# Feed-forward block of an encoder layer: the up projection of two token groups as seven half products, and the down projection as a phase of its own

## The reference

```
h  = h + mixed @ w_out
n2 = rmsnorm(h, ffn_norm)
u  = dwconv3(n2 @ w_up, conv_w, conv_b)      # width 3 along the tokens, each sequence by itself
a, g = split(u, 2)                           # 2816 features each
h  = h + (a * gelu_tanh(g)) @ w_down
gate = sigmoid(rmsnorm(h, ple_norm) @ w_ple_gate)
h  = h + gate * (p @ w_ple)
y  = rmsnorm(h, final_norm)
```

## Time and profile before

| | us |
|---|---|
| median of three runs | 2175.13 |
| lowest, highest | 2174.33, 2176.18 |
| the profiled execution's own time | 2172.85 |
| its span (first to last instruction) | 2171.1 |
| TensorE busy | 2109.8 (97%) |
| VectorE busy | 1531.5 (71%) |
| ScalarE busy | 747.8 (34%) |
| GpSimd busy | 319.2 (15%) |

### The profile page before, as it was taken

One profiled execution on the slowest core, in us unless ns is written; L12 is line 12 of the kernel. 1 busy time (PEld: TensorE's weight loads), 2 busy tenths in 40 slices (PEclk: granted clock), 3 DMA queues, 4 the chain that ended last, 5 costly groups with the idle time before them and its releaser, 6 DMA issues.

```text
span 2171.1 us, 29491 instructions
## 1 busy us (share of the span) xinstructions
PE 2109.8 (97%) x10614; PEld 1712.4 (79%) x10614; DVE 1531.5 (71%) x1985; ACT 747.8 (34%) x1197; POOL 319.2 (15%) x196
## 2 busy tenths in 40 slices
PE   7999999999989999999999999999999999999997
PEld 6788887776767788888888888888888888877785
DVE  6799635777666766677777767777777767778546
ACT  6323214666666721322122212122222212136223
POOL 4122201000011144200000100000100100006101
PEclk9999999999999999999999999999999999999998
DMA  5224357101177331011001000101001000111103
GB/s 179 93 111 154 122 179 172 30 14 29 37 165 164 91 117 36 20 39 39 29 29 39 29 29 31 36 29 39 29 29 37 31 29 29 39 44 38 45 30 117
DMA packets 54460, 139.99 MB, mean 64 GB/s; under 512 B 23296, under 2 KB 23680, under 8 KB 54400
## 3 DMA queue, kind: packets, MB, share of 16 engines
q1 hardware_dynamic: 53536, 138.07, 20.8%
q10 hardware_dynamic: 864, 1.13, 0.1%
HBM read 107.72 MB, written 31.46 MB: 64 GB/s over the span
## 4 chain that ended last, share of the span: by engine, by line
PE 85%; DVE 9%; DMA 2%; issue 2%; ACT 2%; SPq 1%; POOL 0%; DVEq 0%; ACTq 0%
PE ps L307 23%; PE ps L309 23%; PE ps L308 23%; PE ps L1172 4%; PE ps L1143 3%; PE ps L1126 2%; PE ps L1127 2%; DMA KLB<-qkl 1%; DVE qstd L723 1%; PE ps L1189 1%; DVE qt L736 1%; PE ps L1136 1%; DVE WL L303 1%; PE ps L1109 1%; PE ps L1092 1%
## 5 line engine op out<-in xcount | busy, mean ns | idle before, releaser
L307 PE MATMUL ps<-NH,WH 128*128 128x512 f32 x1896 | 744.7, 393 | 17.3 <-DVE WL L706 10.0
L308 PE MATMUL ps<-NL,WH 128*128 128x512 f32 x1896 | 741.6, 391 | 0.0
L309 PE MATMUL ps<-NH,WL 128*128 128x512 f32 x1896 | 741.3, 391 | 0.0
L307 PEld LDWEIGHTS ps<-NH,WH 128*128 128x128 f32 x1896 | 358.4, 189 | 96.1 <-DVE NL L700 8.8
L309 PEld LDWEIGHTS ps<-NH,WL 128*128 128x128 f32 x1896 | 358.1, 189 | 75.2
L308 PEld LDWEIGHTS ps<-NL,WH 128*128 128x128 f32 x1896 | 358.4, 189 | 73.9
L1924 DVE TENSOR_TENSOR H<-H,ps 128x512 f32<-128x512 f32 x480 | 305.5, 683 | 101.8 <-PE ps L309 101.8
L284 POOL TENSOR_TENSOR raw<-raw,gains 128x1024 f32<-128x1024 f32 x76 | 155.6, 2050 | 1161.7 <-DMA raw<-in_w 1161.6
L299 ACT ACTIVATE WH<-raw 128x1024 fp32r<-128x1024 f32 x102 | 107.8, 1057 | 556.8 <-PE ps L309 532.2
L307 PE MATMUL ps<-MH,WH 128*128 128x512 f32 x504 | 196.1, 389 | 0.0
L309 PE MATMUL ps<-MH,WL 128*128 128x512 f32 x504 | 196.1, 389 | 0.0
(11 more groups left out here) (193 smaller groups left out, 2430.6 us busy)
## 6 DMA issues: line engine op xcount, KB each, us to landing
raw<-in_w SPq DMA_DIRECT2D x102, 512.0 KB, 3.3
xst<-in_xT SPq DMA_DIRECT2D x24, 256.0 KB, 3.5
H<-in_xT SPq DMA_DIRECT2D x8, 768.0 KB, 9.0
out_yT<-H SPq DMA_DIRECT2D x24, 256.0 KB, 2.1
Q<-qkh SPq DMA_DIRECT2D x12, 384.0 KB, 6.7
qkh<-oqh SPq DMA_DIRECT2D x5, 768.0 KB, 3.3
qkl<-oql SPq DMA_DIRECT2D x5, 768.0 KB, 4.9
qkh<-obh SPq DMA_DIRECT2D x5, 768.0 KB, 4.8
```

Source lines behind the costliest of these rows:

```text
L307: nc.tensor.matmul(out, wh, xh, start=first, stop=False)
L308: nc.tensor.matmul(out, wh, xl, start=False, stop=False)
L309: return nc.tensor.matmul(out, wl, xh, start=False, stop=last)
```

## The change

**Stage 3 and feed-forward tile 0.** The norm is now applied to H before the split: VectorE multiplies each piece by its gain and the row norm (`normed`), then ScalarE and VectorE split it. `scale_weight` is gone for the up weights. H without the norm is first stored to DRAM (`hT`), since H is overwritten. Tile 0 (content and gate) is still computed whole, the gate's weights being in a place of their own (gate0_h, gate0_l).

**Up projection, j = 1 to 21.** Group 0 of the tokens is computed as before, by four half products: content and gate, each over the upper and the lower half of k. For groups 1 and 2 the halves of k and the pair content and gate make a 2 x 2 block product, made from seven half products P1 to P7 in place of eight. Its weight sums (4 per j) are made by GpSimd and split by ScalarE and VectorE; its token combinations (4 sets of 4 pieces) are made once by GpSimd, in place of pieces of H, and split once. The results are put together in PSUM (two products continue a bank that has been read) and by copies (ScalarE) and additions (VectorE) into u_a and u_g. A half product is 4 k x 3 passes. Weights come from a new array `wu` in quarters of 256 KB.

**Activation.** The product a * gelu(g) of each tile is stored to DRAM (`act`), 768 KB for each j.

**Down projection.** After all up tiles: for each token group, all 22 tiles are summed in PSUM's eight banks, with a weight tile (512 KB) and the group's piece of the activation (256 KB) loaded and split for every pair (group, tile): 66 times. H comes back from `hT` by eight loads of 768 KB in group 0's tiles. Then the group's eight sums are added to H. The embedding's first weights are loaded within group 0.

Cut to its core:

```diff
+DOWN0 = FF0 + 2
+PLE0 = DOWN0 + G * NJ - 2
...
         def s3_sync(sp):
...
+                for m in range(2 * i - 2, 2 * i):
+                    if m >= 0:
+                        sp.wait_ge(h_up, G * (m + 1))
+                        nc.sync.dma_start(a["hT"][m], H[:, m, :]).then_inc(piece_moved[m], 16)
...
+            def normed(g, k):
+                if k == 0:
+                    dve.wait_ge(st_ok, ROW4 + g + 1)
+                dve.wait_ge(piece_moved[k], 16 * (G + 2 + (g if k == LAST_M else 0)))
+                nc.vector.scalar_tensor_tensor(H[:, k, cols(g)], H[:, k, cols(g)], gains[:, 2, k:k + 1], rstd_h[:, cols(g)],
+                                               ALU.mult, ALU.mult).then_inc(n_n, 1)
...
+            for x in range(KT * G):
+                if x + 1 < KT * G:
+                    normed(*pieces[x + 1])
+                low(*pieces[x])
+                if x == 4:
+                    last_merge(2)
...
+        PRODUCTS = [("a", A11, "p_lo", 6, True, False), ("a", A21, "p_lo", 7, True, False), ("a", A22, "p_hi", 7, False, True),
+                    ("a", A12, "p_hi", 6, False, True), ("a", A11, "b11", 0, True, True), ("a", A22, "t4", 1, True, True),
+                    ("s", 1, "t2", 2, True, True), ("s", 0, "t1", 3, True, True), ("s", 2, "t3", 2, False, True),
+                    ("a", A12, "b21", 0, False, True), ("s", 3, "b22", 3, False, True)]
+        X_A11, X_A21, X_A22, X_PLAIN, X_P1, X_P4, X_P6, X_P5, X_P7, X_P2, X_P3 = range(NPROD)
...
         def s4_sync(sp):
+            with sp.Fori(1, LAST_J) as j:
+                sp.wait_ge(prod, products(j, X_A21))
+                load_quarter(sp, j + 1, A21)
+                store_act(j - 1)
+                sp.wait_ge(prod, products(j, X_P1))
+                load_quarter(sp, j + 1, A11)
+                sp.wait_ge(prod, products(j, X_P4))
+                load_quarter(sp, j + 1, A22)
+                sp.wait_ge(prod, products(j, X_P2))
+                load_quarter(sp, j + 1, A12)
+            store_act(LAST_J - 1)
+            sp.wait_ge(prod, products(LAST_J, X_PLAIN))
+            sp.wait_ge(m_st, 16 * LAST_J)
+            load_act(0, 0)
+            load_act(0, 1)
+            sp.wait_ge(prod, products(LAST_J, X_P1))
+            load_down(0, 0)
+            sp.wait_ge(prod, products(LAST_J, X_P2))
+            load_down(0, 1)
+            load_down(0, 2)
+            load_act(0, 2)
+            store_act(LAST_J)
+            load_down(0, 3)
+            load_act(0, 3)
+            sp.wait_ge(prod, products(LAST_J, X_P3))
+            sp.wait_ge(m_st, 16 * NJ)
+            nc.sync.dma_start(rstd_h[:], a["pT"][0:P, :]).then_inc(p_ld, 16)
+            for x in range(2):
+                nc.sync.dma_start(PLE_raw[:, x, :], a["w"][PLE_ROW + x]).then_inc(p_ld, 16)
+            for g in range(G):
+                for j in range(4 if g == 0 else 0, NJ):
+                    load_down(g, j)
+                    load_act(g, j)
+                    if g == 0 and j % 2 == 1 and j < 4 + 2 * KT:
+                        k = (j - 5) // 2
+                        nc.sync.dma_start(H[:, k, :], a["hT"][k]).then_inc(piece_moved[k], 16)
...
         def s4_pool(pool):
+            def weight_sum(j, x):
+                for q in ((A21, A22), (A11,), (A11, A21), (A12,))[x]:
+                    pool.wait_ge(aq_ld[q % 2 ^ (q // 2)], quarter_landed(j, q))
...
+                    pool.wait_ge(prod, products(j - 1, (X_P5, X_P6, X_P7, X_P3)[x]))
...
+                nc.gpsimd.tensor_tensor(out[x][:, x, :], one, two, op).then_inc(s_sum, 1)
...
         def s4_tensor(pe):
+            def product(j, x):
+                if x == X_P4:
+                    pe.wait_ge(combo, combined(j - 1, B_C21))
+                if x == X_P7:
+                    pe.wait_ge(combo, combined(j, B_U2))
+                if x == X_P3:
+                    pe.wait_ge(combo, combined(j, B_C22))
...
+                for k in range(HALF):
+                    xh, xl = operand(name, k)
+                    mm = three_pass(ps[:, bank, :], wh[:, part, cols(k, P)], wl[:, part, cols(k, P)], xh, xl, first and k == 0,
+                                    last and k == HALF - 1, x >= X_P7)
+                mm.then_inc(prod, 1)
...
+            def middle(g, j, slot):
+                tile_ready(g, j)
+                for m in range(KT):
+                    mm = down(g, j, m, slot, False, False)
                 mm.then_inc(w_done, 1)
...
         def s4_scalar(act):
+            with act.Fori(1, LAST_J) as j:
+                front(j)
+                for q in A_ORDER[:3]:
+                    part_high(j + 1, q)
+                for x in range(3):
+                    sum_high(j + 1, x)
+                centre(j, 1)
+                copy(j, C_C11)
+                centre(j, 0)
+                part_high(j + 1, A12)
+                gelu(j)
+                sum_high(j + 1, 3)
...
+                if g < G - 1:
+                    down_high(g + 1, 0)
+                    down_high(g + 1, 1)
+                for m in range(KT):
...
                     nc.scalar.activation(sqe[m % 2][:], H[:, m, cols(g)], ACT.Square).then_inc(f_sq, 1)
+                act.wait_ge(w_done, down_tile(g, LAST_J) + 1)
+                for m in range(KT):
+                    nc.scalar.activation(NH[:, m, cols(g)], H[:, m, cols(g)], ACT.Copy).then_inc(f_hi, 1)
...
         def s4_vector(dve):
+            with dve.Fori(1, LAST_J) as j:
+                front(j)
+                for q in (A11, A21, A22):
+                    part_low(j + 1, q)
+                sum_low(j + 1, 0)
+                taps(j, 1, (0, 1))
+                combine(j, B_C12)
+                taps(j, 1, (2, 3))
+                part_low(j + 1, A12)
+                taps(j, 0, range(4))
+                product(j)
+                for x in range(1, 4):
+                    sum_low(j + 1, x)
...
+            front(LAST_J)
+            down_low(0, 0)
+            taps(LAST_J, 1, (0, 1))
+            combine(LAST_J, B_C12)
+            taps(LAST_J, 1, (2, 3))
+            down_low(0, 1)
+            taps(LAST_J, 0, range(4))
+            product(LAST_J)
```

More of the change, by code:

```diff
@@ L290, in landed, with split_hi @@
             return (n - slot) * 8 + 16
-        def split_hi(act, n, slot, scaled):
+        def split_hi(act, n, slot, scaled, more=0):
             if scaled is None:
@@ L1771, in s4_tensor @@
-            for g in range(G):
+                    pe.wait_ge(r_free, 2 * LAST_C + 3 * second + g + 1)
+                if g == 0:
+                    pe.wait_ge(w_lo, DOWN0)
+                for k in range(KT):
+                    if k == 3 and g < 2:
+                        norm_row(pe, g + 1)
+                    pe.wait_ge(n_lo, KT * g + k + 1)
+                    first, last = k == 0, k == KT - 1
+                    one = three_pass(ps[:, g, :], WH[:, 0, cols(k, P)], WL[:, 0, cols(k, P)], NH[:, k, cols(g)], NL[:, k, cols(g)], first, last)
+                    two = three_pass(ps[:, 3 + g, :], gate0_h[:, cols(k, P)], gate0_l[k // HALF][:, cols(k % HALF, P)], NH[:, k, cols(g)],
+                                     NL[:, k, cols(g)], first, last)
@@ new lines, in s4_tensor, with down @@
+            for x in range(NPROD):
+                product(1, x)
+            with pe.Fori(2, NJ) as j:
+                for x in range(NPROD):
+                    product(j, x)
+            def down(g, j, m, slot, first, last):
+                at = slice(GT * g + P * (m % HALF), GT * g + P * (m % HALF) + P)
+                w = 2 * slot + m // HALF
+                return three_pass(ps[:, END_BANKS[m], :], NH[:, w, at], NL[:, w, at], NL[:, HALF + slot, cols(g)], NH[:, HALF + 2 + slot, cols(g)],
+                                  first, last)
@@ new lines, in s4_vector, with front @@
+            for q in range(4):
+                part_low(1, q)
+            for x in range(4):
+                sum_low(1, x)
+            for n in (3, 1, 2, 4):
+                combo_low(n)
+            taps(0, 1, range(4))
+            taps(0, 0, range(4))
+            product(0)
+            def front(j):
+                for x in (B_U2, B_U3, B_C22, B_C21):
+                    combine(j, x)
+            with dve.Fori(1, LAST_J) as j:
[11 more added lines that the diff above has]
+                    sum_low(j + 1, x)
@@ L2046, in s5_sync @@
             for n in range(PLE0 + 2, NW):
-                load_weight(sp, n, n % 2)
+                load_weight(sp, n, n % 2, row=n - PLE0 + PLE_ROW)
             for g in range(G):
@@ L2374, in layout @@
     tiles += [up(0, 0), up(0, 1)]
+    tiles += [w_down[P * j:P * (j + 1)] for j in range(NJ)]
+    parts = []
     for j in range(1, NJ):
-        tiles += [up(j, 0), up(j, 1), w_down[P * (j - 1):P * j]]
-    tiles.append(w_down[P * (NJ - 1):])
+        content, gate = up(j, 0), up(j, 1)
+        parts += [content[:, :GT], gate[:, :GT], gate[:, GT:], content[:, GT:]]
     for q in range(4):
```

775 lines of the change are left out of this document (442 added, 333 removed).

## The result

The changed kernel takes **2156.98 us** (median of four, 2155.6 to 2159.34), the kernel before 2175.22 beside it: ratio **0.9917**, 95% interval 0.9900 to 0.9934. It is faster, by 18 us; forecast were 38. The time lies inside the range, the forecast is wrong by half of the gain. The profiled execution took 2159.34 us, span 2157.3.

What follows compares the result with a forecast made beforehand. The prediction took TensorE's number of matmuls to bound the kernel. Its terms, -57.1 + 11 + 6 + 9 - 3 - 4 = -38 us, gave 2137 us, with a range of 2118 to 2163.

Steps and rivals of the forecast that it cites:

- Step 1: Up projection, tiles 1 to 21: 132 matmuls in place of 144 at 0.2267 us each, saving 57.1 us.
- Step 2: Up loop: TensorE stays the bound, other engines keep up with smallest margin 1.4 us at P3; zero stall.
- rival A: Up loop stalls a little each time: 1.2 us per tile, 25 us in all, 2162 us; chance 0.15.
- Step 3: Seam from output to up projection: norming and combinations delay the first tile, P4 and P7; +11 us (4 to 25).
- Step 4: Seam from up to down projection: late low parts and loads queued behind the last activation's store; +6 us (2 to 15).
- Step 5: Down phase: no stall per tile, but waits at two group changes of 3.7 and 5.2 us; +9 us (0 to 15).
- Step 6: Old end and tail: waits of the old last two tiles go, -3 us; tail work done earlier, -4 us (-7 to +2).
- B: Down phase bound by its weight loads at a landing of 9.0 us: 50 us, 2187 us; chance 0.07.
- C: Seams are hidden: 10 us in place of 26, giving 2121 us; chance 0.15.
- D: Saving isn't there because the half products' matmuls pace slower: 2194 us; chance 0.03.

Runs made afterwards that it cites:

- e3: Changed kernel with half product P6 computing only 1 of 4 k, 9 of 12 matmuls left out in each of 21 tiles: 2114.07 us.
- e6: Changed kernel with each of GpSimd's four sums of weight quarters done twice in up-loop tiles 2 to 21: 2211.27 us.
- e1: Changed kernel without the 16 token combinations on GpSimd at the start of the up projection, their signals kept: 2143.47 us.
- e2: Changed kernel with the 16 token combinations moved from GpSimd to VectorE, behind the low parts of the first pieces and tile 1's weights: 2152.02 us.
- e5: Changed kernel with only SyncE's DMA issue order changed: activation stores behind weight loads, down tiles' loads earlier at the up-to-down seam: 2148.49 us.
- e8: Changed kernel with 33 matmuls added ahead of P4 of tile 1, where TensorE waited 8.0 us: 2157.34 us.
- e4: Changed kernel with the next group's third tile split earlier at both down-phase group changes, and the second change's root of the sums earlier: 2149.27 us.
- e10: Changed kernel with e2, e4 and e5 together, tile 1's weight sums on VectorE, reordered combinations, and earlier low or high parts of some down tiles: 2126.61 us.
- e12: As e10, with the spread of the first group's norm row issued after 9 instead of 12 matmuls of the last output tile's third group: 2125.93 us.
- e7: Changed kernel with one more 512 KB transfer per tile from SyncE's queue in down-phase groups 1 and 2: 2160.63 us.
- e11: As e10, but combinations split in the changed kernel's order and P4 waiting for all 16: 2122.84 us.

## Why the prediction was wrong

- **Step 1, -57.1:** right. e3 gives 0.2275 us per matmul left out.
- **Step 2, zero stall:** right in size. Its list of margins was not complete: the low part of A21 behind GpSimd's third sum has 2.7 us of cover (e6), and with 3.5 us of delay there rival A comes true, at 2.7 us per tile.
- **Step 3, +11: the term that failed, measured at 24.8.** It failed where it said "some 16 us x 0.7 = 11: it ends near 933", and it took nothing for GpSimd from there on. The price per operation is 1.05 us, and 21 operations meet it. Thirteen of them meet the norming and low parts of the pieces and cost 13.4 us (11 were forecast). The other eight meet the low parts of the four quarters and four sums, which took 13.7 us in place of 5: 8.7 us (0 were forecast). This second part is why P4's wait is 8.0 instead of 1.7. e1 shows it by taking the combinations away, e2 by moving them. The 1.3 us quoted for a norming step and its low part was right (0.66 + 0.60) wherever GpSimd rests.
- **Where step 3's first tile went:** it was to end at 934.4 and ended at 940.8. VectorE began its first norming at 892.3 where 888 was forecast: 2.3 us of that lie before 871, and 1.7 are the half clock at the norm row. Of GpSimd's 13.4 us only 2.4 come on top of the forecast. In the ledger, which leaves out what lies before 871, the first tile has some 12.3 us (8.1 were forecast), P4's wait 7.8 (1.7), the slow matmuls behind it 1.5 (1.6 were forecast for a wait for U2, which did not come), and the wait for AL 2.8 (0). For the last, the prediction saw in step 2 that "the A11 load stands behind" the store, and never put it in the sum for the first tile, whose product comes late (e5).
- **How 0.7 misled:** the Trainium skill's rule (SBUF — State Buffer, "Who interferes with whom") is exclusion for a whole instruction, and the trace bears it out nearly in size: a norming that meets a GpSimd operation ends 0.55 us after it, where it takes 0.74 alone. In the 9.39 us row three of the eight low parts are long, each beside one GpSimd operation: 1.78 us beside the sum of 1.61, and 2.38 beside each of the two scalings that take 4.65 together. The first two of the three, in the kernel before:

```profile
899.50 1.78 DVE L1641 TENSOR_TENSOR NL<-H,NH 128x512 fp32r<-128x512 f32 x1
...
901.20 2.38 DVE L1641 TENSOR_TENSOR NL<-H,NH 128x512 fp32r<-128x512 f32 x1
```

  The low part beside the sum lost 1.10 us, the very price found later. 0.7 was nearly right per microsecond that GpSimd takes beside VectorE (1.05 of 1.67 is 0.63), but the sum multiplied it with GpSimd's time alone (1.3), which makes 0.91 per operation.
- **Half clock:** in the ledger the slow matmuls cost 11.9 us against 3.3 before, of it 5.15, 2.05 and 3.9 at the three places with long waits (of the 5.15, 1.7 at the norm row and about 1 behind short waits at full clock). The sum had no term for it at the new seams. But it is not all a cost of its own: e8 removed one such stretch and gained nothing.
- **Step 4, +6:** 7.9. The waits are the three named (5.8, of which e5 removed 3.8), the rest is clock.
- **Step 5, +9:** 14.9. The mechanism was right (e4, with e10 to e12 leaving nothing of it), the size was not. The first change cost 6.6 us of standstill (with the clock 8) in place of 3.7: the squares, paced by GpSimd's additions, ended 9.3 us after the group and not 7.4, and the third tile's low part then stood 1.4 us behind the eight rests on VectorE, which had not been counted. The second cost 3.7, less than the 5.2 forecast. So most of the overrun is the slow matmuls behind both waits, 3.9 us. The down phase took 382.8 us (1582.2 to 1965.0), above the 375 at which the prediction called itself wrong.
- **Step 6:** old end -4.4 (-3); tail and rest -1.3 (-4): the tail's VectorE wait for the last low parts went, but its final sums stayed as they were.
- **Rivals:** A is out at this load, by 2.7 us of cover; B is out (e7); C had the sign of the seams wrong; D is out (e3). None of them named the true case, which is C's opposite: the seams come to 47.6 us in place of 26. It was in the text all the same, for the first seam, as the upper end of step 3: 25 us if GpSimd's 20 operations of 1.5 us stand in VectorE's way in full. The time lies inside the range, but above the forecast's own band (2127 to 2150) and beside A's 2162 by chance: A's stalls in the loop did not happen.

Open: the 3.5 us of e7, how much of e10's extra 3.8 is real, and why the half clock at the norm row comes in some executions only.

## What to carry to other kernels

Price a helper engine's operation by what it takes from the engine that everything waits for, one operation at a time from a row where both run, not as a share of a time that the helper takes alone, and carry the price to the end of that engine's queue, not to the next event; if its own price there is lower (0.61 against 1.05 us), do the work on it. Where a phase begins or changes, write down each engine's queue up to the first instruction that the bound engine needs, SyncE's included: reordering three such queues gave 16 us, over a quarter of the matmul saving, and with the helper's work moved 36. Test a margin by doubling the cheapest thing in it: a loop with no wait in its trace lost 54 us to sums done twice, with 2.7 us of cover.

## What the runs showed of the hardware that I had not expected

- A VectorE operation with two SBUF inputs that comes up while a GpSimd operation runs on SBUF ends only after it: 1.77 us in place of 0.74 (norming), 1.75 in place of 0.68 (low part), and GpSimd's own takes 1.67 in place of 1.29. It pays to move 16 such operations from GpSimd to a VectorE that is already the bound (e2).
- The granted clock went to 0.5 for 6.8 us after a standstill of 8.0 us (10.2 in e5), for 10.2 after 8.9 (e11) and for 13.7 after 12.7 (e10), and not at all there when matmuls filled the 8.0 (e8). The length of a standstill does not settle it: behind 1.3 us it fell for 3.4 us in nine traces of 13 and not in four, behind some 4 us at the second group change for 6.8 in two and 3.4 in seven.
- The 16 DMA engines at 236 GB/s, 70% busy, still landed 512 KB in 3.7 us (3.2 at 144 GB/s).
